# A two-layer decoder trunk on one NeuronCore: 24 tiles turned by VectorE and an exchange through DRAM instead of by TensorE

## What is computed

```python
# layer 1 (even)
p = rms_norm(h, norm_g) @ w_in
qkv = silu(causal_depthwise_conv(qkv_a, conv_qkv))            # 8 heads x 128
o   = gated_delta_rule(l2_norm(q) * 128**-0.5, l2_norm(k), v, beta, g)
o_a = rms_norm(o, dn_norm_g) * silu(z_a)                      # "delta rule outputs"
glu = glu_b[..., :1024] * sigmoid(glu_b[..., 1024:])          # "GLU products"
c   = layer_norm(causal_depthwise_conv(glu, dw_w) + dw_b)     # 31 taps
o_b = silu(c) * silu(z_b)
o_m = memory_attend(q_m, z_m, ...)
h   = h + concat(o_a, o_b, o_m) @ w_out
# layer 2 (odd)
h   = h + concat(stick_breaking(...), memory_attend(...)) @ w_out2   # of rms_norm(h) @ w_in2
```

## Time and profile before

| | us |
|---|---|
| median of 3 runs | 1323.17 |
| lowest and highest | 1322.9 and 1323.55 |
| the profiled execution, its own time | 1322.03 |
| its span in the trace | 1320.3 |

### The profile page before, as it was taken

One profiled execution on the slowest core, in us unless ns is written; L12 is line 12 of the kernel. 1 busy time (PEld: TensorE's weight loads), 2 busy tenths in 40 slices (PEclk: granted clock), 3 DMA queues, 4 the chain that ended last, 5 costly groups with the idle time before them and its releaser, 6 DMA issues.

```text
span 1320.3 us, 18059 instructions
## 1 busy us (share of the span) xinstructions
PE 1313.2 (99%) x6653; PEld 1117.0 (85%) x6653; DVE 989.5 (75%) x1526; ACT 741.2 (56%) x1159; POOL 105.2 (8%) x103
## 2 busy tenths in 40 slices
PE   9999999999999999999999999999999999999998
PEld 8998899888888888888888888888888888888887
DVE  5557589898898998686666477798788788667563
ACT  6546633476445556576336456847757658554341
POOL 2000301003020100000000020020110200000000
PEclk9999999999999999999999999999999999999999
DMA  9655464555756996666755755765775766977652
GB/s 315 200 174 182 145 196 136 151 177 160 229 172 192 309 283 191 219 196 198 215 176 148 250 172 163 224 206 162 228 211 153 238 196 188 283 212 224 202 191 80
DMA packets 160432, 262.38 MB, mean 199 GB/s; under 512 B 25008, under 2 KB 43353, under 8 KB 160345
## 3 DMA queue, kind: packets, MB, share of 16 engines
q1 hardware_dynamic: 157625, 256.51, 62.6%
q10 hardware_dynamic: 2720, 4.72, 1.1%
HBM read 245.85 MB, written 15.34 MB: 198 GB/s over the span
## 4 chain that ended last, share of the span: by engine, by line
PE 79%; DVE 1%; POOL 0%; issue 0%; DVEq 0%
PE job L1873 49%; PE job L1883 24%; PE mixer L2098 1%; PE mixer L2086 1%; PE mixer L1894 1%; PE mixer L2108 1%; PE mixer L2116 1%; PE mixer L2003 0%; PE mixer L2107 0%; PE mixer L2118 0%; PE mixer L1983 0%; DVE cvr L1632 0%; DVE wlo L1384 0%; PE mixer L2016 0%; PE mixer L1991 0%
## 5 line engine op out<-in xcount | busy, mean ns | idle before, releaser
L1873 PE MATMUL job<-whi,xhi 128*128 128x512 f32 x1532 | 610.7, 399 | 0.0
L1873 PE MATMUL job<-whi,xlo 128*128 128x512 f32 x1532 | 597.3, 390 | 0.0
L1384 DVE TENSOR_TENSOR wlo<-raw,whi 128x1024 fp32r<-128x1024 f32 x431 | 529.1, 1247 | 75.4 <-ACT whi L1042 74.4
L1042 ACT ACTIVATE whi<-raw 128x1024 fp32r<-128x1024 f32 x431 | 444.9, 1055 | 209.5 <-PE job L1883 158.6
L1883 PE MATMUL job<-wlo,xhi 128*128 128x512 f32 x1532 | 409.9, 389 | 0.0
L1883 PEld LDWEIGHTS job<-wlo,xhi 128*128 128x128 f32 x1532 | 287.6, 188 | 60.5
L1873 PEld LDWEIGHTS job<-whi,xhi 128*128 128x128 f32 x1532 | 287.9, 188 | 57.6
L1873 PEld LDWEIGHTS job<-whi,xlo 128*128 128x128 f32 x1532 | 288.0, 188 | 57.4
L1632 DVE SCALAR_TENSOR_TENSOR cvr<-cvr,vt 128x255 f32<-128x255 f32 (+14 forms) x240 | 106.3, 500 | 0.2
L1870 PE MATMUL job<-xhi,whi 128*128 128x256 f32 x376 | 94.1, 288 | 0.4 <-DVE xlo L1429 0.4
L1870 PE MATMUL job<-xlo,whi 128*128 128x256 f32 x376 | 92.1, 283 | 0.0
(11 more groups left out here) (297 smaller groups left out, 964.4 us busy)
## 6 DMA issues: line engine op xcount, KB each, us to landing
raw<-in_od_w_in_dram SPq DMA_DIRECT2D x160, 512.0 KB, 3.8
raw<-in_ev_w_in_dram SPq DMA_DIRECT2D x143, 512.0 KB, 4.1
raw<-in_ev_w_out_dram SPq DMA_DIRECT2D x48, 512.0 KB, 5.3
raw<-in_od_w_out_dram SPq DMA_DIRECT2D x48, 512.0 KB, 5.1
raw<-in_w_mem_kv_dram SPq DMA_DIRECT2D x32, 512.0 KB, 4.7
proj<-turned_blocks SPq DMA_DIRECT2D x48, 128.0 KB, 4.6
turned_blocks<-proj SPq DMA_DIRECT2D x8, 512.0 KB, 4.5
turned_weights<-mix SPq DMA_DIRECT2D x16, 192.0 KB, 4.8
```

The lines of the kernel that those rows point to most:

```text
L1042: act(whi[:, c % RING, :, :], raw[:, c % RAWS, :, :], ACT.Copy).then_inc(s_hi, 1)
L1384: vec.tensor_tensor(wlo[:, c % RING, :, :], raw[:, c % RAWS, :, :], whi[:, c % RING, :, :].bitcast(F32), ALU.subtract).then_inc(s_lo, 1)
L1873: mm(pj[j % 2][n][:, :], x[:, s, cols], h, start=first, stop=False)
```

## The change

Four things are done, and the plan is made anew with them.

- The first 12 of the 16 fills of layer 2 (blocks `H_TURNED` 0 to 2), the four GLU tiles of the second half (`GLU_TURNED + 1`) and all eight tiles of delta rule output (`DN_TURNED`, two blocks) go through `lt`, `xw`, `xr` in place of TensorE. That is 24 tiles, 48 turns, in six more exchanges (the seventh new block in the DRAM tensor, `GLU_TURNED`, is not used: the first half of the GLU stays with TensorE).
- ScalarE copies these tiles from the exchanged block instead of from PSUM; for the fills of layer 2 VectorE makes `xlo` in two instructions of 128 columns a tile instead of one of 256.
- Tap 0 of the convolution moves to ScalarE (new step `cv0`).
- Steps that followed move in the plan: the chunks of convolution by some positions, `lnc` 2 and 3 from position 110 to 112, the layer norm and the memory attention of layer 1 by 2 to 4 positions, the reload of x (`xload`) from positions 132 to 137 to positions 135 to 140, `xr` of block 2 from 136 to 139.

```diff
-        return s, last + [("wait", g)] + [(("d7", h), .5 + .3 * g) for h in range(h0, h0 + 4)]
+        e = DN_TURNED + g
+        return s, last + [(("lt", e), 0), (("xw", e), 2), (("xr", e), 3)] + [(("d7", h), .5) for h in range(h0, h0 + 4)]
...
-        stream(2, after(J_GLU[g] + 1) + 6 * g, [(("glu", g), 2 + g)] + [(("gT", ct), 1) for ct in range(4 * g, 4 * g + 4)])
+        start = after(J_GLU[g] + 1) + 6 * g
+        s = [(("glu", g), 1), (("lt", GLU_TURNED + g), 1), (("xw", GLU_TURNED + g), 2), (("xr", GLU_TURNED + g), 3)] if g else [(("glu", g), 2)]
+        stream(2, start, s + [(("gT", ct), .5 if g else 1) for ct in range(4 * g, 4 * g + 4)])
...
+            if d == 0:
+                left.pop(0)
+                stream(2, p, [(("cv0", pr), 0)])
...
+    for b in range(3):
+        turn_job(H_TURNED + b, CH0[J_OM + 1 + b])
...
+        if b < 3:
+            stream(5, CH0[J_OM + 1 + b] + (5, 6, 6)[b] + k % 4 // 2, [(("xt", F_H + k), 0)])
+            continue
+        stream(5, CH0[J_ODIN] + 4 + (k - 12) // 2, [(("xt", F_H + k), 0)])
...
             def do_dnB(h):
                 sc.wait_ge(s_back, h + 1)
                 if h >= 4:
-                    sc.wait_ge(s_owp, h - 3)
+                    sc.wait_ge(*exchanged(DN_TURNED, 1))
...
             def do_d7(h):
-                sc.wait_ge(s_owp, h + 1)
-                act(mix[:, h, :], M[banks("d7", h)[0]][:, 0:S], ACT.Copy, scale=gain("ev_dn_norm_g", 0)).then_inc(s_mixa, 1)
+                e = DN_TURNED + h // 4
+                sc.wait_ge(*exchanged(e))
+                act(by_quarter(mix[:, h, :]), landed(e).rearrange("p (a h t j) -> p h t a j", a=4, h=4, t=T)[:, h % 4], ACT.Copy,
+                    scale=gain("ev_dn_norm_g", 0)).then_inc(s_mixa, 1)
...
+            def do_cv0(pr):
+                if pr:
+                    sc.wait_ge(s_cv, 2 * (TAPS - 1) * pr)
+                for ct in (2 * pr, 2 * pr + 1):
+                    sc.wait_ge(s_gt, ct + 1)
+                    col = V_DW + 8 * (TAPS - 1) + ct
+                    act(cvr[:, ct, :], cvr[:, ct + 2, :], ACT.Identity, bias=gain("ev_dw_b", ct), scale=vt[:, col:col + 1]
+                        ).then_inc(s_c0, 1)
...
             def do_lt(e):
-                j = TURNED[e]
-                ve.wait_ge(*evac_done(j))
+                if e >= DN_TURNED:
+                    ve.wait_ge(s_ow, 8 * (e - DN_TURNED) + 8)
+                elif e >= GLU_TURNED:
+                    ve.wait_ge(s_glu, e - GLU_TURNED + 1)
+                else:
+                    ve.wait_ge(*evac_done(TURNED[e] if e < H_TURNED else J_OM + e - H_TURNED))
...
-                vec.transpose(stage[e].rearrange("p (b m j) -> p m b j", b=4, j=32), landed(e)).then_inc(s_jt, 1)
+                vec.transpose(stage[e].rearrange("p (b m j) -> p m b j", b=4, j=32), unturned(e)).then_inc(s_jt, 1)
```

More of the change, by code:

```diff
@@ L257, in make_plan @@
     for j in range(len(JOBS)):
[L258 removed]
+        late = 5 if j in (J_GLU[1], J_GLU[1] + 1) else 0 if J_OM <= j < J_ODIN or j == len(JOBS) - 1 else 1 if j else 3
         stream(-1, CH0[j + 1] + late, [(("evac", j), 0)])
@@ L489, in landed, with unturned @@
         def landed(e):
-            return slot(PSLOT[TURNED[e]])
+            if e == DN_TURNED + 1:
+                return tiles(16)
+            return slot(PSLOT[TURNED[e]] if e < H_TURNED else e - H_TURNED if e < GLU_TURNED
+                        else PSLOT[J_GLU[e - GLU_TURNED]] if e < DN_TURNED else PSLOT[J_GLU[1]])
+        def unturned(e):
+            if e < H_TURNED or GLU_TURNED <= e < DN_TURNED:
+                return landed(e)
+            if e >= DN_TURNED:
+                return tok[:, :, 0:2, :].rearrange("p h c n -> p h (c n)")
+            return hid[:, :, 512 * (e - H_TURNED):512 * (e - H_TURNED) + 512]
         def head_tile(v, h):
@@ L1081, in do_xt @@
             def do_xt(n):
+                if F_H <= n < F_H + 12:
+                    e, h = divmod(n - F_H, 4)
+                    sc.wait_ge(*exchanged(H_TURNED + e))
+                    fill_wait(n)
+                    act(by_quarter(xhi[:, SLOT[n], :]), head_tile(landed(H_TURNED + e), h), ACT.Copy, scale=xt_gain(n)
+                        ).then_inc(s_xh, 1)
+                    return
                 sc.wait_ge(s_xp, turned(n))
@@ L1428, in do_xt @@
                 ve.wait_ge(s_xh, n + 1)
+                if F_H <= n < F_H + 12:
+                    e, h = divmod(n - F_H, 4)
+                    for t in range(T):
+                        ins = vec.scalar_tensor_tensor(
+                            out=by_quarter(xlo[:, SLOT[n], :])[:, t], in0=head_tile(landed(H_TURNED + e), h)[:, t],
+                            scalar=xt_gain(n), in1=by_quarter(xhi[:, SLOT[n], :].bitcast(F32))[:, t], op0=ALU.mult, op1=ALU.subtract)
+                    ins.then_inc(s_xl, 1)
+                    return
                 vec.scalar_tensor_tensor(out=xlo[:, SLOT[n], :], in0=M[banks("xt", n)[0]][:, 0:S], scalar=xt_gain(n),
@@ L1690, in do_zb @@
                     ve.wait_ge(s_xl, F_OM)
+                    ve.wait_ge(*exchanged(H_TURNED + 2, 1))
                 src = proj[32 * a:32 * a + 32, slot, :, :].rearrange("p t (h n) -> p h t n", h=4)
@@ L2050, in do_d5e @@
                 mm(M[1][:, 0:128], aq[:, 2 * (h % 4) + 1, 1, :], dw[h % 2][:, 2, :], start=True, stop=True).then_inc(s_5ep, 1)
-            def do_d7(h):
-                pe.wait_ge(s_ow, 2 * h + 2)
-                take("d7", h)
-                for t in range(T):
-                    ins = turn(M[banks("d7", h)[0]][:, 128 * t:128 * t + 128], tok[:, h % 4, t, :])
-                ins.then_inc(s_owp, 1)
             def do_gT(ct):
+                if ct >= 4:
+                    return
                 i = ct // 4
```

81 lines of the change are left out of this document (49 added, 32 removed).

## The result

| | before | changed |
|---|---|---|
| median | 1323.1 us (4 runs, 1322.9 to 1323.55) | **1332.01 us** (4 runs, 1331.24 to 1334.19) |
| ratio to before | | 1.0068, 95% interval 1.0055 to 1.0082 |
| profiled execution, own time | 1322.03 | 1332.71 |
| its span, mean granted clock | 1320.3, 1.0 | 1330.8, 0.995 |

What follows compares the result with a forecast made beforehand. TensorE, busy 1313.2 of 1320.3 us, was taken as the bound. The terms, 6.3 - 0.5 - 1.5 - 0.3 = 4.0 us less, gave 1318.0 for the profiled execution and a 1319.2 us median, range 1316.6 to 1321.8.

Steps and rivals of the forecast that it cites:

- The turns, 5.9 + 0.4: On TensorE: removing the turns saves 5.9 us, and a wait at the first delta rule tile another 0.4.
- The first `d4x`, 0.5: Second group's inverse chain has no slack, so TensorE, arriving earlier, waits 0 to 1.0 us; 0.5 taken.
- The fourth mask, 0.5 gained: TensorE's 0.5 us wait for this GpSimd mask goes, as `lnc` 2 and 3 no longer hold it.
- The sums on GpSimd, 2.0: `lnc` 2 and 3, behind late taps, delay the sixth mask; TensorE waits 1.4 to 3.6 us, 2.0 taken.
- SyncE's queue, 0.3: Held store of block 4 delays later loads to chunk 150's weight load; 0.3 us expected, 0 to 2.6.
- The slower rival: SyncE held twice by landings over 11.5 us, making chunk 150 late; 1326.8 us at landings of 12, chance 0.08.
- The cases of more given back: Larger waits at mask, `d4x`, DMA stretch or layer 2: 1323.6 us with the first three, one or two 1320.5 to 1322; chance 0.17.
- wrong altogether: Sign against the whole forecast: granted clock below full anywhere, or TensorE's busy time not down by some 6 us.
- Right that it just fits: Chunk 150's load is ready by 489.2 us against 489.3 wanted, in a stretch with DMA 94% busy at 305 GB/s.
- VectorE and ScalarE at nothing: Both run well ahead of TensorE, smallest lead 2.8 us at chunk 105, so their changed work costs nothing.
- layer 2's exchanges at nothing: Each new exchange has 13.6 us against 10.8 at the median, so costs nothing; 2.4 us at most.

Runs made afterwards that it cites:

- a_fill14: The changed kernel with 14 identity matmuls, results never read, on TensorE ahead of the `d4x` that waits for the sixth mask; 1329.94 us.
- a_both: The changed kernel with four exchange semaphores, loads of blocks 2 and 3 three positions later, and `lnc` 2 and 3 behind the sixth mask; 1317.48 us.
- a_early: The changed kernel, still with three semaphores, with the loads of blocks 2 and 3 at positions 136 and 137 in place of 139 and 140; 1327.98 us.
- b_late: The kernel before with the loads of blocks 2 and 3 three positions later, at 139 and 140; 1329.66 us.
- a_lock: The changed kernel with VectorE starting a `wlo` only once GpSimd has done the two sums and the sixth mask; 1328.85 us.
- a_best: a_both_inv with the second group's copies `d7` one position nearer to the loads of their block; 1317.81 us.
- a_sem4: The changed kernel with four semaphores for the exchanges in place of three, queue order untouched; 1330.21 us.
- a_lnc: The changed kernel with the sums `lnc` 2 and 3 one position later, behind the sixth mask on GpSimd; 1326.28 us.
- a_both_inv: a_both with the second group's `inT` and all that follows one position later; 1316.54 us.
- b_lnc112: The kernel before with `lnc` 2 and 3 moved from position 110 to 112, ahead of the sixth mask; 1322.65 us.
- a_sem4_late: The changed kernel with four exchange semaphores and the loads of blocks 2 and 3 three positions later, behind those of block 4; 1323.29 us.

## Why the prediction was wrong

*The turns, 5.9 + 0.4.* Right to 0.35 of 6.3: 5.95 by chunk starts (1.3 + 0.9 + 0.95 + 2.8), the first wait included.

*The first `d4x`, 0.5.* Right in its mechanism, mis-sized: 1.2, outside its range of 0 to 1.0. The chain came 1.1 us earlier, TensorE 2.3. I had counted only the GLU turns (1.0) as TensorE's gain on the chain; group 0's 1.3 were won ahead of it too, and the chain did not follow that gain.

*The fourth mask, 0.5 gained.* Right: 0.7.

*The sums on GpSimd, 2.0.* Right place, mis-sized: 3.54, at the upper end of its 1.4 to 3.6. The taps ran beside nothing (1.55) and ended at 377.5, but the sums ran beside `wlo` and took 3.30 in place of the row's 1.62. I had the lock between the two engines before my eyes for the taps (0.78 against 1.40 a pair) and applied it to them alone.

*SyncE's queue, 0.3.* **This is the step that failed.** It followed the hold as it happened (block 2's loads landed after 6.4 us, the store after 3.0) to the wrong reader: the weight load of chunk 150. In the changed kernel that chunk was split by 495.4 and taken at 504.4, with 9 us to spare. The data that the queue carries had a reader of its own, the gate of block 4 that ends in `xlo` for chunk 146, with 1.3 us of slack; TensorE waited 8.0 us there. It started block 2's loads too early as well, at 462 against 465.7. I costed the steps that the change *added* to the queue and not those whose *contents* the queue delays. The slower rival named this stretch and this hold, and 0.08 for it, but by the same wrong reader and from landings over 11.5 us; the two landings that it asks for took 6.4 and 3.0 us, and the kernel was slower all the same.

*The clock: left out.* Nowhere did the sum ask what TensorE does after a wait. 4.5 us of the 10.65 are this (1.6 + 2.9). The 1.6 is shown by a_fill14; the 2.9 is read from the clock and its going with the wait. The cases of more given back took a wait at its length (and by the prediction's own terms one or two of them give 1319.7 to 1323.9, not 1320.5 to 1322), and the text did say that a granted clock below full would make it wrong altogether.

*Bandwidth.* Right that it just fits: in a_both DMA is at 100% of this stretch, with no wait that matters.

*VectorE and ScalarE at nothing, layer 2's exchanges at nothing.* Right: between chunks 150 and 222 no wait appeared, and VectorE's total moved by 2.3 us.

## What to carry to other kernels

When a change moves steps in a shared queue, list every item behind them with its own reader and that reader's slack; the item with the most slack is easy to find and says nothing. A wait for another engine is priced with what runs beside that engine at that time, and with the clock that TensorE has afterwards: here a wait of 3.0 us cost 4.8, one of 3.5 cost 5.1, one of 8.0 cost 10.9, and one of 1.9 cost itself. A change that "loses" can hold a gain: the same edit with four semaphores in place of three, eight loads and two sums in another place, is 0.4% faster than the kernel before.

## What the runs showed of the hardware that I had not expected

- The clock fell to 1.2 GHz behind single waits of 3.0 (a_early), 3.5, 4.0 (b_late) and 8 us in a kernel that is otherwise 99% busy, and did not behind 1.9 (a_lock) and 1.8 us (a_best, chunk 144). The price of the same wait of 3.5 us differed, 1.6 us in one profile and 2.6 in another (a_sem4). Matmuls that do nothing, in the wait, kept it at 2.4 GHz (a_fill14).
- Two sums of 128x256 on GpSimd: 1.59 to 1.62 us with VectorE idle or in one-input instructions, 3.30 to 3.35 in a_lnc, a_both and the changed kernel, where `wlo` ran beside them, 2.53 in a_both_inv and a_best, where `wlo` ran beside a part of them, and 1.80 in b_lnc112 beside taps that were slowed themselves.
- The landing of one 512 KB store depends on what left before it: 3.0 us where SyncE had been held and issued nothing for 4.6 us, 3.3 to 5.1 with weight loads alone just ahead (a_both, a_best, a_sem4_late, a_both_inv), 5.5, 8.0, 8.5 and 9.7 us where loads of exchanged blocks stood in front (a_sem4, before, b_late, a_early).
